# The fourth stick-breaking sample step, moved from the third attention pair's steps into the fourth pair's

## The chip, the cores and the metric

The kernel runs as one program on one core of a Trainium2 chip. The metric is the device time of one execution in microseconds (us); the kernel before was run three times, and its median is 1700.19 us.

## The reference, cut to what matters

One inference step of a hybrid encoder layer, for one prompt of 1024 rows and for eight samples of 16 rows with 512 cached positions each. All of it is float32, D_MODEL is 1024.

```
h = rmsnorm(x); z = h @ W_in
MLA, 8 heads:            softmax attention over latents, for samples over cache + own rows
retention, 4 heads
stick-breaking, 4 heads: log_beta = log_sigmoid(z), log_keep = log_sigmoid(-z) where key before query
                         between = reverse cumsum(log_keep) - log_keep
                         a = exp(log_beta + between); out = a @ v
x += concat(heads) @ W_out
x += memory cross-attention(rmsnorm(x))
x += ConvFFN(rmsnorm(x)); final rmsnorm
```

For the samples, stick-breaking runs over the caches `cache_sb_k` and `cache_sb_v`, and MLA over `cache_mla_ckv` (the latents) and `cache_mla_kpe` (the rotary keys).

## The kernel before, in words

**Stages.** The program runs in this order: the input projection with retention beside it, an attention stage written as numbered steps, the samples' latent attention, then the output projection, memory attention, ConvFFN and the last norm. The change lies in the attention stage, which ends at the latent attention.

**The steps.** `STEPS` (L212 to L223) is the one list from which every engine takes its order. It starts with ten "sb" steps, stick-breaking of the prompt. Then come four MLA pairs (two heads each), numbered 0 to 3 in the code and first to fourth here, of five steps each: `PACKS` names the tiles of 128 queries that one step takes, (7,), (6, 0), (5, 1), (4, 2), (3,). Between them stand four "sbs" steps. Each of these is the stick-breaking attention of two samples, for all heads, and takes one score tile where an MLA step takes two. `SB_S_AFTER` says behind which step of which pair each stands: `(2, 1): 3` puts the last one behind the second step of the third pair. The step numbers t of the attention stage are in the kernel before: 23 and 24 the third pair's first two, 25 the last sbs step, 26 to 28 the rest of the third pair, 29 to 33 the fourth pair.

**The pipeline over t.** TensorE's loop (L2609) does in turn t: the scores of step t, the transposes of the probabilities of t-1, the values of t-2. Between them it puts chunks of the next pair's projections (`STEP_CHUNKS`, L304; a pair has 11, spread over the four first MLA steps of the pair before; the fourth pair has none to place). An sbs step issues `sample_scores` (L2462, L2466) in turn t, five transposes (L2480) in turn t+1, `values` (L2497) in turn t+2, and in turn t+3 two transposes, `turn_sums` (L2512), and a wait for `sb_picked`. ScalarE takes the exponentials (L1143) or, for an sbs step, two sigmoids (L1134, L1135), each change of function with a table load; it copies the first group of every transposed head (L1154) and the outputs (L1166, L1170), and picks the turned sums (L1180). VectorE takes the row maxima and masks (L1742, L1745, L1736), the normalisation (L1767, L1771) or, for sbs, the scan and product (L1755, L1760), the second group's copy (L1782), and evacuates the query chunks (L1795).

**What is loaded where.** The sbs steps read their caches from four blocks of `z` (`cache_k`, `cache_v`; two transfers of 1 MB per step). The same blocks are later filled for the latent attention: `lat_v` of samples 2 to 7 and the rotary keys `lat_pe` of samples 0 to 3. The rest of the rotary keys goes where the projections' inputs were, and the latents `lat_k` and `lat_v` of samples 0 and 1 go into the buffers of the third pair. SyncE's queue (SP) issues all of these in one fixed order:

```
            sp.wait_ge(pv_done, SB_S_STEP[-1] + 1)
            for b in range(4):
                load_rotary(b)
            for b in range(2, DB):
                load_values(b)
            sp.wait_ge(proj_done, NCK * NP)
            ...
            sp.wait_ge(pv_done, END[NP - 2])
            for b in range(DB):
                sp.dma_start(lat_k[b], io["lat"][b, 0]).then_inc(lat_in[b], 16)
                if b < 2:
                    load_values(b)
```

`pv_done` counts the finished `values`, one per step, and `SB_S_STEP[-1]` is the number of the last sbs step. Where the "..." stands, the other four samples' rotary keys and `w_v` are issued. A `load_rotary` is two transfers (L850), a `load_values` one (L845), a `lat_k` one (L866). Behind them SP issues the first two weight blocks of the output projection (L761); GpSimd (POOL) splits a block into a high and a low part (L918, L921).

**Who needs them.** In turn t = N_STEPS = 34, `latent_scores(0)` (L2567, L2573) waits for `lat_in` of samples 0 and 1, 64 each, so for both samples' two rotary transfers, values and latents. TensorE takes this ahead of the values of step 32. `N_STEPS` stays 34 wherever an sbs step stands.

Of the kernel before, what the change touches and what calls it, by code (L numbers as in the profile page):

```python
# [207 lines left out]


PACKS = ((7,), (6, 0), (5, 1), (4, 2), (3,))  # L210
SB_S_AFTER = {(0, 2): 0, (1, 0): 1, (1, 3): 2, (2, 1): 3}
STEPS = [("sb", p, tiles) for p in range(2) for tiles in (PACKS[4:] + PACKS[:4] if p == 0 else PACKS)]  # L212
N_SB = len(STEPS)
FIRST, END, SB_S_STEP = [], [], []
for _i in range(NP):
    FIRST.append(len(STEPS))
    for _k, _tiles in enumerate(PACKS):
        STEPS.append(("mla", _i, _tiles))
        if (_i, _k) in SB_S_AFTER:
            SB_S_STEP.append(len(STEPS))  # L220
            STEPS.append(("sbs", SB_S_AFTER[_i, _k], (PAST // P,)))
    END.append(len(STEPS))
# [2843 lines left out]
```

## Time and profile before

| | |
|---|---|
| median of 3 runs | 1700.19 us (1700.18 to 1700.97) |
| the profiled execution's own time | 1700.53 us |
| its span in the trace | 1698.7 us |
| TensorE busy | 1673.5 us (99%) |
| VectorE, ScalarE, GpSimd busy | 1059.9, 530.7, 499.9 us |
| granted TensorE clock, mean | 0.999 |

The span runs from the first to the last instruction of the profiled execution; its own time is 1.8 us longer. "Busy" is the share in which an engine has an instruction under way. TensorE's matmuls overlap, so a matmul's duration is longer than the distance from its start to the next one's. In the tables, "idle before" is the time that an engine stood still ahead of an instruction, and the arrow names what ended it.

### The profile page before, as it was taken

The page shows a single profiled execution, that of the slowest core. Times are in us where ns is not written, and L with a number is a line of the kernel's source. Part 1 is how long each engine was busy: PE and PEld are TensorE (multiplying, and loading weights), DVE is VectorE, ACT ScalarE, POOL GpSimd, SP SyncE. Part 2 cuts the span into 40 slices and gives each one's busy share as a digit, 9 for nine tenths or more (in the row PEclk, how much of TensorE's full clock was granted, in tenths as well). Part 3 has the DMA queues.
Part 4 walks back from the last instruction along what each step waited for, and adds up shares of the span by engine and source line. Part 5 has one row for each costly group of instructions (what it writes and reads, how often), then busy time and mean ns, then how long its engine had stood idle before and what let it go on. Part 6 is the DMA issues. An engine that isn't in the chain of part 4 may idle for free.

```text
span 1698.7 us, 26502 instructions
## 1 busy us (share of the span) xinstructions
PE 1673.5 (99%) x10487; PEld 1544.3 (91%) x10487; DVE 1059.9 (62%) x1438; ACT 530.7 (31%) x960; POOL 499.9 (29%) x231
## 2 busy tenths in 40 slices
PE   9999999999999999999999999999999999999998
PEld 8899879766667799998999999999999999999997
DVE  7483477896666655446677656565655656565566
ACT  7220122586566541215333120211203021120222
POOL 2683142000000123420333333433334333343332
PEclk9999999999999999999999999999999999999999
DMA  5322121320222324316211111111111111111113
GB/s 207 92 86 81 52 69 38 110 75 24 77 86 69 113 78 138 107 38 266 90 38 50 38 47 39 37 49 37 48 38 37 49 37 49 37 37 49 38 47 112
DMA packets 36333, 119.41 MB, mean 70 GB/s; under 512 B 6048, under 2 KB 9344, under 8 KB 33952
## 3 DMA queue, kind: packets, MB, share of 16 engines
q1 hardware_dynamic: 33952, 108.89, 20.0%
q10 hardware_dynamic: 2304, 9.44, 1.6%
q8 instruction: 56, 0.92, 0.2%
q14 instruction: 21, 0.17, 0.0%
HBM read 100.86 MB, written 15.17 MB: 68 GB/s over the span
## 4 chain that ended last, share of the span: by engine, by line
PE 93%; DVE 3%; ACT 1%; issue 1%; POOL 1%; DMA 0%; SPq 0%; DVEq 0%; ACTq 0%; POOLq 0%
PE scores L2118 35%; PE bank L2118 35%; PE scores L2423 3%; PE bank L2480 3%; PE scores L2214 2%; PE bank L2504 2%; PE bank L2127 1%; PE scores L2136 1%; PE scores L2445 1%; PE bank L2534 1%; PE bank L2775 1%; PE bank L2538 1%; PE scores L2753 1%; PE bank L2497 1%; DVE kbuf L1755 1%
## 5 line engine op out<-in xcount | busy, mean ns | idle before, releaser
L918 POOL TENSOR_TENSOR w_hi<-w_raw,zero 128x1024 fp32r<-128x1024 f32 x96 | 187.4, 1952 | 1104.2 <-PE bank L2118 466.8
L2118 PE MATMUL scores<-act_hi,w_hi 128*128 128x384 f32 x920 | 310.2, 337 | 0.9 <-POOL w_lo L921 0.9
L2118 PE MATMUL scores<-act_lo,w_hi 128*128 128x384 f32 x920 | 309.1, 336 | 0.0
L2118 PE MATMUL scores<-act_hi,w_lo 128*128 128x384 f32 x920 | 309.1, 336 | 0.0
L921 POOL TENSOR_TENSOR w_lo<-w_raw,w_hi 128x1024 fp32r<-128x1024 f32 x96 | 252.5, 2631 | 7.5
L2046 DVE TENSOR_TENSOR x<-bank,x 128x384 f32<-128x384 f32 x216 | 120.5, 558 | 103.6 <-PE bank L2118 103.6
L2118 PE MATMUL bank<-act_hi,w_hi 128*128 128x384 f32 x544 | 183.7, 338 | 0.9 <-POOL w_lo L921 0.9
L2118 PE MATMUL bank<-act_hi,w_lo 128*128 128x384 f32 x544 | 182.8, 336 | 0.0
L2118 PE MATMUL bank<-act_lo,w_hi 128*128 128x384 f32 x544 | 182.8, 336 | 0.0
L2118 PEld LDWEIGHTS scores<-act_hi,w_hi 128*128 128x128 f32 x920 | 173.0, 188 | 2.5 <-POOL w_lo L921 1.5
L2118 PEld LDWEIGHTS scores<-act_lo,w_hi 128*128 128x128 f32 x920 | 173.0, 188 | 0.0
L2118 PEld LDWEIGHTS scores<-act_hi,w_lo 128*128 128x128 f32 x920 | 173.0, 188 | 0.0
L2020 DVE SCALAR_TENSOR_TENSOR conv<-ext,consts,conv 128x1168 f32<-128x1168 f32 x44 | 117.6, 2673 | 79.4 <-ACT conv L1421 79.4
L2118 PE MATMUL bank<-s_lo,w_hi 128*128 128x384 f32 (+2 forms) x454 | 152.7, 336 | 0.0
L2118 PE MATMUL bank<-s_hi,w_hi 128*128 128x384 f32 (+2 forms) x454 | 152.7, 336 | 0.0
L2118 PE MATMUL bank<-s_hi,w_lo 128*128 128x384 f32 (+2 forms) x454 | 152.6, 336 | 0.0
L1432 ACT ACTIVATE s_hi<-conv 128x1024 fp32r<-128x1024 f32 x20 | 21.2, 1060 | 344.2 <-DVE conv L2029 344.2
L2118 PEld LDWEIGHTS bank<-act_hi,w_hi 128*128 128x128 f32 x544 | 102.3, 188 | 2.1 <-POOL w_lo L921 1.2
L2118 PEld LDWEIGHTS bank<-act_lo,w_hi 128*128 128x128 f32 x544 | 102.3, 188 | 0.0
L2118 PEld LDWEIGHTS bank<-act_hi,w_lo 128*128 128x128 f32 x544 | 102.3, 188 | 0.0
L2022 DVE SCALAR_TENSOR_TENSOR conv<-ext,consts,conv 128x1168 f32<-128x1168 f32 x44 | 83.1, 1888 | 7.0 <-DVE conv L2020 4.2
L2118 PEld LDWEIGHTS bank<-s_hi,w_hi 128*128 128x128 f32 x454 | 85.3, 188 | 0.3
(402 smaller groups left out, 3101.2 us busy)
## 6 DMA issues: line engine op xcount, KB each, us to landing
w_raw<-wstream SPq DMA_DIRECT2D x106, 512.0 KB, 3.6
x_blk<-xT ACTq DMA_DIRECT2D x8, 576.0 KB, 4.7
x_mid<-x_blk ACTq DMA_DIRECT2D x8, 576.0 KB, 3.1
x<-x_mid SPq DMA_DIRECT2D x4, 1152.0 KB, 5.5
z<-cache_k SPq DMA_DIRECT2D x4, 1024.0 KB, 5.4
z<-cache_v SPq DMA_DIRECT2D x4, 1024.0 KB, 7.3
mk_c<-mk_c SPq DMA_DIRECT2D x4, 1024.0 KB, 11.7
mv_c<-mv_c SPq DMA_DIRECT2D x4, 1024.0 KB, 13.7
```

The lines of the kernel that those rows point to most:

```text
L918: pool.tensor_tensor(w_hi[:, k], w_raw[:, k], zero[:].unsqueeze(2).to_broadcast([P, KB, P]), ALU.add).then_inc(w_rounded, 1)
L921: pool.tensor_tensor(w_lo[:, k], w_raw[:, k], w_hi[:, k].bitcast(F32), ALU.subtract).then_inc(w_split, 1)
L1432: act.activation(dst[:, 0:TP], conv[:, 0, 0:TP], ACT.Copy)
L1755: own_v(dve.tensor_tensor_scan(keep[:, ::-1], keep[:, ::-1], ones[:, 0:1].to_broadcast([P, w]), 1.0, ALU.mult, ALU.mult))
L2020: own_v(dve.scalar_tensor_tensor(c, ext[:, ab, 1:EXT - 1], conv_tap(m + NFF * ab, 1), c, ALU.mult, ALU.add))
L2022: dve.scalar_tensor_tensor(c, ext[:, ab, 2:EXT], conv_tap(m + NFF * ab, 2), c, ALU.mult, ALU.add).then_inc(conv_done, 1)
L2046: dve.tensor_tensor(x[:, m, frames(c)], bank[6 + q % 2][:, 0:CH], x[:, m, frames(c)], ALU.add).then_inc(d_evac, 1)
L2118: mm = pe.matmul(out, w[:, k, at + kb], x(kb), start=first and kb == 0 and n == 0, stop=last and kb == n_kb - 1 and n == 2)
L2214: mm = pe.matmul(bank[c][:, 0:CH], w[:, 0, kb], x[:, at, frames(c)], start=i == 0 and n == 0, stop=i == KB - 1 and n == 2)
L2423: mm = pe.matmul(S[hh][:, at:end], q_pass[i % 2][:, hh, tile(j)], k_pass[i % 2][:, hh, at - first:end - first], start=True, stop=True)
L2480: mm = pe.transpose(bank[4 + g % 2][:, tile(b)], taken(t, hh)[:, tile(4 * k + b)], ident[:])
L2504: mm = pe.matmul(bank[6][64 * hh:64 * hh + 64, tile(n)], v, probT[:, t % 2, hh, at + P * b:at + P * b + P], start=b == 0, stop=b == j)
```

## The change

The last sbs step stands behind the second step of the fourth pair.

```diff
 PACKS = ((7,), (6, 0), (5, 1), (4, 2), (3,))
-SB_S_AFTER = {(0, 2): 0, (1, 0): 1, (1, 3): 2, (2, 1): 3}
+SB_S_AFTER = {(0, 2): 0, (1, 0): 1, (1, 3): 2, (3, 1): 3}
 STEPS = [("sb", p, tiles) for p in range(2) for tiles in (PACKS[4:] + PACKS[:4] if p == 0 else PACKS)]
```

With it `SB_S_STEP[-1]` goes from 25 to 30, `END[NP - 2]` from 29 to 28, and the steps from there are numbered: 25 to 27 the rest of the third pair, 28 and 29 the fourth pair's first two, 30 the sbs step, 31 to 33 the rest of the fourth pair. The two waits of SP that are quoted above are for `pv_done` at 31 and at 28, where they were for 26 and 29. Nothing else in the code is changed.

## Rows read from the trace of the kernel before

**Rows 1.** The page: engines, and the chain that ended last, by line.
```profile
PE 1673.5 (99%) x10487; PEld 1544.3 (91%) x10487; DVE 1059.9 (62%) x1438; ACT 530.7 (31%) x960; POOL 499.9 (29%) x231
PE 93%; DVE 3%; ACT 1%; issue 1%; POOL 1%; DMA 0%; SPq 0%; DVEq 0%; ACTq 0%; POOLq 0%
```

**Rows 2.** Windows: length, PE, PEld, DVE, ACT, POOL busy (instructions), PEclk, DMA share, GB/s.
```profile
538.50:572.40 33.90, 33.90 (x276) 24.75 (x273) 26.42 (x60) 20.43 (x53) 0.56 (x1) 1.00 0.51 164
572.40:603.00 30.60, 29.63 (x211) 21.29 (x209) 17.36 (x38) 16.06 (x36) 7.90 (x4) 1.00 0.13 35
603.00:700.00 97.00, 97.00 (x578) 96.11 (x577) 51.23 (x44) 24.39 (x27) 36.13 (x14) 1.00 0.38 124
```

**Rows 3.** TensorE's timeline around the sbs step: start, us, engine, line, operation.
```profile
504.49 0.45 PE L2538 MATMUL bank<-cq_hi,wq_hi 128*128 128x384 f32 x1 [0.27 <-ACT k_pass L1206]
...
509.48 1.10 PE L2480 MATMUL bank<-ident,prob 128*128 128x128 f32 x8 [0.34 <-ACT probT L1154]
...
521.24 1.16 PE L2545 MATMUL bank<-w_pass,z 128*128 128x128 f32 x8 [0.37 <-DVE q_pass L1795]
...
531.41 0.60 PE L2497 MATMUL bank<-sv_tok,probT 128*64 128x256 f32 x4
531.95 0.71 PE L2550 MATMUL bank<-q_pass,w_pass 64*128 64x128 f32 x4
...
533.55 0.38 PE L2512 MATMUL bank<-ident,probT 128*128 128x128 f32 x2
533.76 1.04 PE L2480 MATMUL bank<-ident,prob 128*128 128x128 f32 x8
```

**Rows 4.** ScalarE's timeline: the table loads on either side of the sigmoids.
```profile
509.36 1.28 ACT L1134 ACT_TABLE_LOAD   x1
...
516.86 1.28 ACT L1143 ACT_TABLE_LOAD   x1
```

**Rows 5.** SP's timeline: the loads in the order of their issue.
```profile
532.06 3.59 SPq L850 DMA_DIRECT2D z<-kpe_c  x8
535.68 2.79 SPq L845 DMA_DIRECT2D z<-lat  x6
538.52 3.68 SPq L850 DMA_DIRECT2D lat_pe<-kpe_c  x8
542.25 0.42 SPq L862 DMA_DIRECT2D w_v<-w_v  x1
...
552.34 0.43 SPq L866 DMA_DIRECT2D lat_k<-lat  x1
552.82 0.43 SPq L845 DMA_DIRECT2D lat_v<-lat  x1
553.29 2.97 SPq L866 DMA_DIRECT2D lat_k<-lat  x6
```

**Rows 6.** DMA issues: w_v; lat_k of sample 1; the last lat_k (size, us to landing).
```profile
w_v<-w_v SPq DMA_DIRECT2D x1, 256.0 KB, 4.3
...
lat_k<-lat SPq DMA_DIRECT2D x1, 256.0 KB, 3.5
...
lat_k<-lat SPq DMA_DIRECT2D x1, 256.0 KB, 6.1
```

**Rows 7.** TensorE's timeline from the last pair's last step to the first latent scores.
```profile
565.95 1.13 PE L2423 MATMUL scores<-k_pass,q_pass 128*128 128x512 f32 x2
...
572.44 1.02 PE L2567 MATMUL scores<-lat_k,q_abs 128*128 128x512 f32 x2
```

**Rows 8.** TensorE's first 32 matmuls (timeline); eight transposes of the fourth pair (chain).
```profile
1.09 5.52 PE L2184 MATMUL bank<-ones 128*128 128x128 f32 x32 [1.09 <-DVE eps L1480]
...
567.08 0.87 PE bank L2480 x8
```

**Rows 9.** GpSimd's first weight split; TensorE's first matmul that reads a split block.
```profile
571.85 1.89 POOL L918 TENSOR_TENSOR w_hi<-w_raw,zero 128x1024 fp32r<-128x1024 f32 x1 [263.86 <-DVE prob L1771]
...
602.95 0.60 PE L2214 MATMUL scores<-mix,w_hi 128*128 128x384 f32 x2
```

## The prediction

> **What bounds the kernel now.** I read the page first. TensorE is busy for 99% of the span and holds 93% of the chain that ended last, DMA 0% of it [rows 1]. So a microsecond taken from or added to TensorE's order is a microsecond of the end, unless TensorE was standing there anyway. The windows by stage come next [rows 2]: over the fourth pair, 538.5 to 572.4, TensorE is busy in all of 33.90 us. In the latent attention up to 603 it rests for 0.97 us of 30.60, and behind that not at all. Nothing after the changed place has a reserve that would swallow a delay. The fourth pair has no hole either, though it has no projection chunks: moving a step into it fills nothing.
>
> TensorE's timeline around the sbs step has the only rests near it: 0.27 us for an evacuated key chunk, 0.34 us between two transposes, 0.37 us for an evacuated query chunk [rows 3]. Last I read SP's timeline [rows 5]. The first load for the latent attention starts at 532.06, and the sbs step's values end at 531.41 + 0.60 = 532.01 [rows 3]. That end releases it, 0.05 us later. In the code this wait is `pv_done` at the last sbs step plus one.
>
> **The change part by part.** TensorE's instructions stay the same in number and shape: they move by five steps. So do the two sigmoids, their two table loads, the scan, the product and the copies.
>
> *1. The third pair without the sbs step.* The rest of 0.37 us at 521.24 lies behind the second of the table loads, 1.28 us at 516.86 [rows 3, 4]: ScalarE is late with the exponentials, VectorE with the normalisation behind them, and so with the query chunk. Without the step this goes. The rest of 0.27 us stands ahead of it and stays. I take -0.4 us; the bounds are 0 and -0.98, all three rests.
>
> *2. The fourth pair with it.* The 0.34 us belongs to the sbs turn itself, where two heads' transposes follow each other without scores between them, and moves along: 0. The table load back to the exponentials was followed by TensorE work on two projection chunks, which are missing there. What hides it is one head's scores and the values of step 29; my estimate, from the durations in the third pair, is that the exponential is just ready when TensorE asks. If not, it costs at most one table load, +1.28 us. I take 0. The turned sums and the wait for `sb_picked` fall in turn 33, after the release of the loads; a delay there is swallowed by term 3.
>
> *3. The loads behind the sbs step.* This is the large term. The release moves from turn 27 to turn 32, and with it everything behind it in SP's queue: eight rotary transfers, six of values, eight rotary, `w_v`, and then latents and values of samples 0 and 1, 27 transfers, before `latent_scores(0)` may start. The later wait, for the third pair's values, is then long met, so nothing pauses the queue.
>
> What TensorE still has to do behind the release: before, turn 33 and one head's transposes took 572.44 - 565.95 = 6.49 us [rows 7]; the turned sums add 533.76 - 533.55 = 0.21 us [rows 3]. The values end 0.06 us after the start of the next matmul (532.01 against 531.95). That leaves 6.64 us.
>
> What the loads need: `w_v` is issued 542.25 - 532.06 = 10.19 us after the first load and lands 4.3 us later, so at 14.5 us [rows 5, 6]. Up to there the sequence is the one of before. Four transfers of 256 KB follow. For their rate I take the second burst: `lat_k` of sample 1 landed at 552.34 + 3.5 = 555.8. The last `lat_k` was issued some 0.43 us before the end of its group of six, at 553.29 + 2.97 - 0.43 = 555.8, and landed 6.1 us later, at 561.9 [rows 5, 6]. Seven transfers in 6.1 us are 0.87 us each. So the fourth lands at 14.5 + 4 x 0.87 = 18.0 us. TensorE rests for 18.0 + 0.05 - 6.64 = **11.4 us**. It has rested nowhere near as long before.
>
> Bounds: the last of the four is issued at about 10.19 + 0.43 x 4 = 11.9 us at the earliest, and if it found the engines as free as sample 1's `lat_k` did (3.5 us) it would land at 15.4, a rest of 8.8 us. If all four ran as slowly as 1 us each, it would be 11.9 us. The value nearer to the upper end is the likelier, since `w_v` already took 4.3 us in a queue that was behind.
>
> *4. TensorE's clock after the rest.* No stretch of this trace has a rest of this length in mid-kernel, so the nearest row is the program's start: the first 32 matmuls of 128x128 took 5.52 us, where eight transposes of the same shape later take 0.87 us of the chain [rows 8], which is 3.5 us for 32. The difference is 2.0 us, though the granted clock of that stretch is given as 1.00. I take **+2.0 us** for the first matmuls behind the rest, which are as dense (latent scores, two steps' values). Bounds: 0, and twice the start's loss, 4.0.
> The Trainium skill, "TensorE: Matmul & The Clock Gate", section "Part 1: The HAM clock gate", says that the gate lets only half of the pulses through when the engine has been idle, and opens once it is busy again. By it the sum has this term; without it the sum would be 2.0 us lower.
>
> *5. What lies further back.* SP's output-projection weights were issued from 556.65 on. In the changed queue they stand behind six more `lat_k`; at 0.87 us for each 256 KB the first 512 KB have landed 18.0 + 8 x 0.87 = 25.0 us after the first load, which starts at 572.44 - 6.64 + 0.05 = 565.85, so at 590.9. GpSimd's first split, which before started at 571.85 on a VectorE result, waits for them. TensorE asks for a split block at 602.95 + 11.4 = 614.4 [rows 9]. Between the two lie 23 us, for a split of which the first half takes 1.89 us: 0. The latents of samples 2 and 3 land 1.7 us behind, while TensorE has the scores of two samples and the values of two steps to do: 0. All later loads hang on TensorE's progress and move with it.
>
> **Sum.** -0.4 + 0 + 11.4 + 2.0 = +13.0 us. The profiled execution took 1700.53 us (span 1698.7 and 1.8 around it), the median is 1700.19, 0.3 lower. From the median this gives 1713.2 us, 0.8% slower. A measurement of this kernel can tell about 0.2%, 3.4 us, from no change.
>
> **The rivals.**
> *A, the clock does not fall* (chance 0.18). The rest is there, but the engine comes back at full rate. For it speaks that the granted clock reads 1.00 in every stretch, even where the first matmuls were slow. Against it, those slow matmuls themselves. 1700.2 - 0.4 + 11.4 = 1711.2 us.
> *B, the fourth pair misses its cover* (0.06). The exponentials behind the sigmoids come a table load too late, and the sums' turn too: up to 1.3 us and a rest of 0.4 us more, with the clock term 1715.0. For it speaks the thin cover in term 2; against it, that the same steps in the third pair rested only where a projection chunk asked.
> *C, not slower: the loads come in time* (0.05). The place is the wait of `latent_scores(0)`. It decides from the point where the fourth 256 KB transfer lands within 6.64 us of the release; then only term 1 is left, 1700.2 - 0.4 = 1699.8, at most 1699.2. Issuing 27 transfers took SP about 12 us of its own time in the trace, so this needs a release that does not move, a change that does not do to SP's queue what the code says. The 0.05 us between the values' end and the first load speaks against that.
> The forecast itself, stall and slow start together, has 0.71.
>
> **The numbers.** The predicted time is the forecast's, 1713.2 us. The range takes in rival A, with the earlier landing (rest 9.6 instead of 11.4: 1709.4), and on the other side rival B with a somewhat slower clock return (1716.5). I set 1709.0 to 1716.5. The rest of 0.2 is C and the corners of the bounds. Slower by over 0.2% are the forecast, A and B: 0.95. Within 0.2% is nearly all of C: 0.04. Faster by over 0.2% has no mechanism: 0.01.
>
> **What the profile after would show.** SP's first rotary load should start about 34 us later, near 565.5, with no pause between `w_v` and the first `lat_k`. TensorE's latent scores should show an idle time of about 11 us ahead of them, released by a DMA, and start near 583.5; the step should be the largest wait of TensorE in the whole trace. The matmuls behind it should be about twice as far apart for some microseconds. The rest of 0.37 us behind the sigmoids should be gone from the third pair, and from 603 on every stage should have its length of before. The forecast is wrong if the idle time ahead of the latent scores is under 8 us, if another wait of over 1 us appears in the fourth pair, or if the first output-projection matmul waits for a weight split.

## The result, and the profile after

The changed kernel takes 1713.26 us (median of 5 runs, 1712.75 to 1714.78), the kernel before, measured beside it, 1700.39 us (1700.18 to 1700.97). The ratio is 1.0077, with a 95% interval from 1.0063 to 1.0091: 12.9 us slower. 1713.2 was forecast.

The profiled execution of the changed kernel is the slowest of the five, at 1714.78 us with a span of 1713.0; against the profiled one of before that is 14.25 us. The page, first its span, then the lines of [rows 1]:

```profile
span 1713.0 us, 26502 instructions
PE 1675.1 (98%) x10487; PEld 1545.5 (90%) x10487; DVE 1061.2 (62%) x1438; ACT 530.5 (31%) x960; POOL 500.0 (29%) x231
...
PE 92%; DVE 3%; ACT 1%; issue 1%; SPq 1%; POOL 1%; DMA 1%; DVEq 0%; ACTq 0%; POOLq 0%
```

The counts are those of before; TensorE's busy time is 1.6 us more, which the low clock below accounts for. What is new is SP's queue and the DMA in the chain that ended last, with 1% each. TensorE's three largest waits in the changed kernel, by their sum (what was waited for: us in all, times, the longest):

```profile
PE scores L2567 <- DMA lat_v<-lat: 12.6, 1, 12.6
PE bank L2480 <- ACT probT L1154: 2.2, 5, 0.9
PE scores L2118 <- POOL w_lo L921: 1.7, 2, 0.9
```

One wait explains nearly all. Its place in TensorE's timeline, from the last sbs step's values to the latent scores (answers to [rows 3] and [rows 7]):

```profile
563.02 1.95 PE L2497 MATMUL bank<-z,probT 128*64 128x256 f32 x16
564.80 0.60 PE L2497 MATMUL bank<-sv_tok,probT 128*64 128x256 f32 x4
565.33 1.12 PE L2423 MATMUL scores<-k_pass,q_pass 128*128 128x512 f32 x2
...
571.17 1.09 PE L2480 MATMUL bank<-ident,prob 128*128 128x128 f32 x8
584.88 2.05 PE L2567 MATMUL scores<-lat_k,q_abs 128*128 128x512 f32 x2 [12.61 <-DMA lat_v<-lat]
586.72 0.63 PE L2567 MATMUL scores<-z,q_abs 128*128 128x128 f32 x2
587.28 1.95 PE L2573 MATMUL scores<-z,q_pe 64*128 64x512 f32 x8
```

And SP's timeline, the answer to [rows 5]:

```profile
565.44 4.05 SPq L850 DMA_DIRECT2D z<-kpe_c  x8
569.53 3.71 SPq L845 DMA_DIRECT2D z<-lat  x6
573.29 3.67 SPq L850 DMA_DIRECT2D lat_pe<-kpe_c  x8
577.01 0.42 SPq L862 DMA_DIRECT2D w_v<-w_v  x1
577.47 0.43 SPq L866 DMA_DIRECT2D lat_k<-lat  x1
577.95 0.43 SPq L845 DMA_DIRECT2D lat_v<-lat  x1
578.42 0.43 SPq L866 DMA_DIRECT2D lat_k<-lat  x1
578.89 0.43 SPq L845 DMA_DIRECT2D lat_v<-lat  x1
```

The values end at 564.80 + 0.60 = 565.40, the first load starts 0.04 us later, and 27 loads go out without a pause, where before there were 8.8 us between `w_v` and the first `lat_k`. The last stretch of the chain in order of time shows where the latest of them landed, 578.89 + 5.74 = 584.63:

```profile
578.89 5.74 DMA lat_v<-lat
584.63 0.25 issue
584.88 2.47 PE scores L2567 x4
```

The windows over the rest and behind it, columns as in [rows 2] (the seventh is the granted clock):

```profile
565.00:572.00 7.00, 7.00 (x66) 5.13 (x62) 5.37 (x14) 4.55 (x16) 0.00 (x0) 1.00 0.47 127
572.00:583.00 11.00, 0.26 (x3) 0.03 (x1) 0.00 (x0) 0.95 (x2) 0.00 (x0) 0.63 0.95 279
584.00:585.00 1.00, 0.12 (x1) 0.15 (x1) 0.00 (x0) 0.00 (x0) 0.00 (x0) 0.50 1.05 383
587.00:588.00 1.00, 1.00 (x4) 0.56 (x5) 0.00 (x0) 0.00 (x0) 0.00 (x0) 0.50 1.04 416
588.00:589.00 1.00, 1.00 (x8) 0.46 (x4) 0.00 (x0) 0.00 (x0) 0.00 (x0) 0.74 1.10 430
589.00:590.00 1.00, 1.00 (x22) 0.88 (x20) 0.70 (x2) 0.00 (x0) 0.00 (x0) 1.00 0.61 238
```

The clock fell to 0.50, that is 1.2 of 2.4 GHz, while TensorE stood still. It reads 0.74 on average between 588 and 589, so it came back at about 588.5, when the engine had been at work again for 3.6 us. Half of these 3.6 us is the loss: from the first latent scores to the values of step 32 it took 589.16 - 584.88 = 4.28 us; before it was 574.90 - 572.44 = 2.46.

The difference of the two profiled executions adds up. The latent scores start 12.78 us later than by the distance of before (0.93 us behind the transposes at 571.17). The low clock costs 1.82. The stretch between the last two old landmarks, the query chunk behind the rest of 0.27 us and the last step's transposes, is shorter by 0.91 (571.51 - 504.49 = 67.02 before, 571.17 - 505.06 = 66.11 after). And the attention stage begins 0.57 us later (505.06 against 504.49), which lies ahead of anything that was changed. 12.78 + 1.82 - 0.91 + 0.57 = 14.26 us. Nothing is left over for the stages behind. TensorE's waits from 700 us on are the same six in both traces, 3.9 us in all.

### The profile page after: what moved, and what is told of

It reads as the page before. It is cut to its first block, busy times and chain, and to the rows that moved or that the text cites. A ratio compares the mean times of both kernels' runs of the same rounds, so it can differ in the third digit from the quotient of the medians.

```text
span 1713.0 us, 26502 instructions
## 1 busy us (share of the span) xinstructions
PE 1675.1 (98%) x10487; PEld 1545.5 (90%) x10487; DVE 1061.2 (62%) x1438; ACT 530.5 (31%) x960; POOL 500.0 (29%) x231
## 4 chain that ended last, share of the span: by engine, by line
PE 92%; DVE 3%; ACT 1%; issue 1%; SPq 1%; POOL 1%; DMA 1%; DVEq 0%; ACTq 0%; POOLq 0%
PE scores L2118 35%; PE bank L2118 35%; PE scores L2423 3%; PE bank L2480 2%; PE scores L2214 2%; PE bank L2504 2%; PE bank L2127 1%; PE scores L2136 1%; PE scores L2445 1%; PE bank L2534 1%; PE bank L2538 1%; PE bank L2775 1%; PE scores L2753 1%; PE scores L2567 1%; PE bank L2497 1%
## 5 line engine op out<-in xcount | busy, mean ns | idle before, releaser
L1432 ACT ACTIVATE s_hi<-conv 128x1024 fp32r<-128x1024 f32 x20 | 21.2, 1060 | 344.1 <-DVE conv L2029 344.1
## 6 DMA issues: line engine op xcount, KB each, us to landing
mv_c<-mv_c SPq DMA_DIRECT2D x4, 1024.0 KB, 13.7
```

Of the source, the lines that this page charges most:

```text
L1432: act.activation(dst[:, 0:TP], conv[:, 0, 0:TP], ACT.Copy)
```

## The experiments

The theory: the whole loss hangs on SP's queue, since the loads of the latent attention wait behind the last sbs step. The rivals: the sbs step costs something in its new place by itself; the clock is not what makes the first latent scores slow; the bytes, not their order, decide. All times are medians. The kernel before, measured beside each, had 1700.35 to 1700.42 us.

### The loads that are free go first

```diff
-            sp.wait_ge(pv_done, SB_S_STEP[-1] + 1)
-            for b in range(4):
-                load_rotary(b)
-            for b in range(2, DB):
-                load_values(b)
             sp.wait_ge(proj_done, NCK * NP)
             ...
+            sp.wait_ge(pv_done, SB_S_STEP[-1] + 1)
+            for b in range(4):
+                load_rotary(b)
+            for b in range(2, DB):
+                load_values(b)
```

The "..." stands for the free loads, which are unchanged: rotary keys of samples 4 to 7, `w_v`, then all `lat_k` and the `lat_v` of samples 0 and 1.

> The changed kernel, with SP's order altered: the loads that don't use the cache blocks (rotary keys of samples 4 to 7, w_v, all lat_k, lat_v of samples 0 and 1) are issued ahead of the wait for the last sbs step, the rest behind it. Theory (the cost is SP's queue behind one wait): behind the release only four rotary transfers are needed for the first latent scores; they land some 3.7 us after it, within the 6.6 us that TensorE still works. No wait on a DMA, no drop of the clock, and only the local gain stays: 1699.5 us, from 1699.2 to 1700.4. Rival (the sbs step in the fourth pair costs by itself): well above 1700.4. Rival (the amount of data behind the release decides): 1705 or more.

Measured: 1699.99 us (1699.36 to 1703.49, 11 runs), ratio 1.0001 [0.9992, 1.001]. The 12.9 us are gone with the sbs step still in the fourth pair: TensorE's timeline has the latent scores at 571.24, with no idle time ahead of them. That is the theory's result, and both rivals fall for this place. But seven runs lie at 1699.4 to 1700.1 and four at 1701.0 to 1703.5, so something else costs now and then. The profiled run (1701.04) shows it. VectorE's and GpSimd's timelines of this kernel:

```profile
579.33 2.66 DVE L1894 TENSOR_SCALAR prob<-prob,row_sum 128x640 f32<-128x640 f32 x1
...
584.21 2.32 DVE L1894 TENSOR_SCALAR prob<-prob,row_sum 128x640 f32<-128x640 f32 x1
...
588.74 0.55 DVE L1894 TENSOR_SCALAR prob<-prob,row_sum 128x640 f32<-128x640 f32 x1
```

```profile
577.32 1.89 POOL L918 TENSOR_TENSOR w_hi<-w_raw,zero 128x1024 fp32r<-128x1024 f32 x1 [269.61 <-DMA w_raw<-wstream]
579.29 2.35 POOL L921 TENSOR_TENSOR w_lo<-w_raw,w_hi 128x1024 fp32r<-128x1024 f32 x1
581.59 2.15 POOL L918 TENSOR_TENSOR w_hi<-w_raw,zero 128x1024 fp32r<-128x1024 f32 x1
583.82 2.35 POOL L921 TENSOR_TENSOR w_lo<-w_raw,w_hi 128x1024 fp32r<-128x1024 f32 x1
```

The two long normalisations start 0.04 and 0.39 us after a GpSimd instruction does (579.29 and 583.82) and end 0.35 us after that one ends (581.99 against 581.64, 586.53 against 586.17). The other five of the seven meet no split; the third shown takes 0.55. TensorE waited 1.8 us for the two in all. In the kernel before, GpSimd started at 571.85 [rows 9] and was done at 580.46, just before the first of the seven, and each of them took 0.55. Here the weights are issued behind the released loads, the split starts 5.5 us later and falls into the normalisations. The Trainium skill, "SBUF — State Buffer", section "SBUF: two separate sides", says that VectorE and GpSimd share one pair of ports as an exclusive lock: a GpSimd instruction, and a VectorE instruction in a two-port mode or with two inputs from SBUF (then only beside a GpSimd instruction that reads SBUF), shut each other out for the whole instruction of the one that starts first. The trace agrees in the times: the end of each long instruction follows the end of GpSimd's, and GpSimd's next one, which begins while the first of them is still under way, takes 2.15 us instead of 1.89. Whether the normalisation runs in such a mode, no row here shows.

### Only the release moves

```diff
-            sp.wait_ge(pv_done, SB_S_STEP[-1] + 1)
+            sp.wait_ge(pv_done, 31)
```

> The kernel before, with one number changed: SP's wait ahead of the first rotary load is for pv_done at 31 instead of 26. The sbs step stays in the third pair. Theory: the queue alone makes the loss. TensorE waits about 12 to 13 us for the latents (19.2 us from release to landing as in the changed kernel, 6.4 us of work left), the clock term of 1.8 comes on top, and the local gain of 0.9 is missing: 1714.3 us, from 1712.5 to 1715.5. Rival (the sbs step's new place costs): 1700.4.

Measured: 1714.37 us (1713.49 to 1715.31), ratio 1.0083 [1.0068, 1.0099]. The step stood in its old place and the loss was there, 1.1 us more of it than in the changed kernel; the local gain of 0.9 us is missing here. It is the reverse of the first experiment; together they show the queue to be both enough and necessary. The wait of the profiled run:

```profile
582.59 2.05 PE L2567 MATMUL scores<-lat_k,q_abs 128*128 128x512 f32 x2 [10.47 <-DMA lat_v<-lat]
```

It is shorter than the 12 to 13 us expected, and the low clock behind it cost 2.52 us, not 1.8 (the table further down), so the time agrees with the expectation in part by luck.

### TensorE kept busy through the rest

```diff
+                if t == N_STEPS:
+                    pe.wait_ge(kv_evac, evacuated(NP - 1, NCK - 1, "act"))
+                    for _ in range(90):   # 45 in the second kernel
+                        pe.matmul(bank[7][:, 0:P], ident[:], ones[:], start=True, stop=True)
                 if t >= N_STEPS:
                     latent_scores(t - N_STEPS)
```

> The changed kernel, with 90 matmuls of 128x128 (identity by ones, into a free bank, read by nothing) ahead of the first latent scores: about 9.8 us of TensorE's rest of 12.6 us are filled. Theory (the first matmuls behind the rest are slow because the clock fell): the latent scores start when they did, the granted clock stays 1.00, and from there to the values of step 32 it takes 2.5 us instead of 4.3: 1.8 us less, 1711.4 us. Rival (they are slow for another reason, as data that still arrives): 1713.3.

Measured: 1719.54 us (1719.04 to 1720.06), far from the 1711.4 expected. I had taken one float32 matmul for one instruction, and it is two: 90 became 180 and filled more than the rest.

```profile
571.20 20.26 PE L2624 MATMUL bank<-ones,ident 128*128 128x128 f32 x180
591.29 1.02 PE L2567 MATMUL scores<-lat_k,q_abs 128*128 128x512 f32 x2
```

The time says nothing on the question, but the trace does: the clock read 1.00, and from these latent scores to the next values it took 2.46 us, as before the change. The second kernel had half of the filling.

> The changed kernel with 45 instead of 90 of the filling matmuls. With 90 the trace had 180 instructions of 0.11 us each, 20.3 us, longer than the rest itself, so the time said nothing; 45 take 10.1 us and leave about 2 us of the rest of 12.6. Theory (the clock had fallen): the latent scores start when the last needed transfer has landed, as in the changed kernel, the granted clock stays 1.00, and from them to the values of step 32 it takes 2.5 us instead of 4.3: 1711.4 us, 1.8 us less. Rival (the first matmuls are slow because transfers still run beside them, or the start after any rest costs that): 1713.3.

Measured: 1712.17 us (1711.66 to 1713.28), ratio 1.0069 [1.0055, 1.0083]: 1.1 us less than the changed kernel, where 1.8 were expected. Its trace:

```profile
571.36 10.21 PE L2624 MATMUL bank<-ones,ident 128*128 128x128 f32 x90
583.23 1.10 PE L2567 MATMUL scores<-lat_k,q_abs 128*128 128x512 f32 x2 [1.66 <-DMA lat_v<-lat]
...
597.68 0.77 PE L2655 MATMUL bank<-ident,prob 128*128 128x128 f32 x5 [0.95 <-DVE prob L1894]
```

The latent scores still waited for the DMA, and behind that wait they ran at full rate: 585.76 - 583.23 = 2.53 us to the values, against 4.28. Transfers still ran beside them (the DMA share was 1.04 from 583 to 585), so these do not slow TensorE, nor does a wait of 1.66 us; in the changed kernel, where the same stretch was slow, the clock read 0.50. In the profiled run a part of the gain was given back by the meeting of VectorE and GpSimd, 0.95 us.

### All behind the release, in the order of need

```diff
             sp.wait_ge(pv_done, SB_S_STEP[-1] + 1)
-            for b in range(4):
-                load_rotary(b)
-            for b in range(2, DB):
-                load_values(b)
-
             sp.wait_ge(proj_done, NCK * NP)
-            for b in range(4, DB):
-                load_rotary(b)
-            sp.dma_start(w_v[:], io["w_v"]).then_inc(sample_in, 16)
-
             sp.wait_ge(pv_done, END[NP - 2])
             for b in range(DB):
+                load_rotary(b)
                 sp.dma_start(lat_k[b], io["lat"][b, 0]).then_inc(lat_in[b], 16)
-                if b < 2:
-                    load_values(b)
+                load_values(b)
+            sp.dma_start(w_v[:], io["w_v"]).then_inc(sample_in, 16)
```

> The changed kernel, all loads still behind the last sbs step's values, but sample by sample (rotary, latents, values), w_v last. The bytes behind the release are the same. Theory (what counts is what stands ahead of the fourth needed transfer): eight transfers instead of 27, issued in 3.7 us and landed 7 to 8 us after the release; a rest of 0 to 1.5 us, no drop of the clock, 1700.5 us, from 1699.4 to 1702. Rival (the bytes in all decide): the rest stays near 12 us and the time at 1713.

Measured: 1704.67 us (1702.38 to 1707.45, 11 runs), ratio 1.0024 [1.0015, 1.0033]. The two waits that matter, from TensorE's timeline:

```profile
572.31 1.10 PE L2559 MATMUL scores<-lat_k,q_abs 128*128 128x512 f32 x2 [0.86 <-DMA lat_v<-lat]
...
598.31 1.33 PE L2643 MATMUL bank<-ident,prob 128*128 128x128 f32 x5 [4.80 <-DVE prob L1886]
```

The first is as expected, 0.9 us where 12.6 were, with the same bytes behind the same release: the order decides, not the amount. The time missed the expectation (1699.4 to 1702). In the profiled run, at 1707.36 one of the longest, the second wait is the reason. The weights came last in this order too, GpSimd split from 588.06 to 597.89, and two normalisations (L1886 here) took 2.14 and 2.31 us; VectorE's instruction on `mixed` between them took 3.50 us instead of 1.35. And TensorE's clock fell in this wait too, though no DMA was waited for:

```profile
603.00:604.00 1.00, 1.00 (x5) 0.51 (x5) 0.00 (x0) 0.00 (x0) 0.00 (x0) 0.55 0.00 0
```

It reads 0.50 from 598 to 603. From the transposes behind the wait to the next ones TensorE took 605.13 - 598.31 = 6.82 us, where the same stretch took 4.67 in the kernel before: 2.15 us on top of the 4.8.

### The step one turn earlier, two earlier, one later

```diff
-SB_S_AFTER = {(0, 2): 0, (1, 0): 1, (1, 3): 2, (3, 1): 3}
+SB_S_AFTER = {(0, 2): 0, (1, 0): 1, (1, 3): 2, (3, 0): 3}   # and (2, 4), and (3, 2)
```

> The last sbs step behind the fourth pair's first step, one turn earlier than in the changed kernel. Theory: the release comes one turn, 7.3 us, earlier; TensorE's rest shrinks from 12.6 to 5.3 us, the clock still falls (1.8 us): 1700.4 - 0.9 + 5.3 + 1.8 = 1706.6 us, from 1704.5 to 1707.5. Rival (the place in the fourth pair costs, not the loads): as the changed kernel, 1713.

> The last sbs step behind the third pair's last step, two turns earlier than in the changed kernel. Theory: some 21 us of TensorE's work lie behind the release, more than the 19.2 us that the loads take: no rest, 1700.0 us, from 1699.4 to 1701. If the local gain of 0.9 us comes from leaving the projection chunks, it shows here, unless this place has a wait of its own.

> The last sbs step behind the fourth pair's third step, one turn later than in the changed kernel. Theory: about 1 us of work is left behind the release, a rest of about 18.3 us, the clock term as before: 1719.6 us, from 1718 to 1721. Rival (the rest is bound by something that doesn't move with the release): 1713.

Measured, with the profiled runs' numbers (start of the first load; idle time ahead of the latent scores; from the first load to the latent scores; what the stretch from these to the second value group, 5.63 us before, took more; how long of it the granted clock read 0.50):

| last sbs step behind | first load | idle | load to scores | slower by | at 0.50 | median |
|---|---|---|---|---|---|---|
| (2, 4) | 551.14 | 0 | 21.2 | 0 | 0 | 1700.65 (1700.18 to 1701.07) |
| (3, 0) | 557.92 | 3.89 | 17.95 | 2.83 | 5.8 | 1706.96 (1706.03 to 1707.75) |
| (3, 1), the change | 565.44 | 12.61 | 19.44 | 1.82 | 3.6 | 1713.26 |
| (3, 2) | 570.66 | 16.25 | 18.00 | 2.47 | 5.1 | 1719.77 (1719.53 to 1719.92) |
| (2, 1), late release | 565.58 | 10.47 | 17.01 | 2.52 | 5.2 | 1714.37 |

The price of the clock is in every row half of the time that it stood at 0.50, to within 0.1 us, and does not follow the length of the rest. The windows in which it came back, of (3, 0), (3, 2) and the late release (the seventh column is its mean over half a microsecond):

```profile
581.50:582.00 0.50, 0.50 (x12) 0.50 (x10) 0.47 (x1) 0.00 (x0) 0.50 (x1) 0.84 0.08 33
593.50:594.00 0.50, 0.50 (x10) 0.50 (x10) 0.37 (x2) 0.00 (x0) 0.00 (x0) 0.78 0.39 131
587.50:588.00 0.50, 0.50 (x9) 0.50 (x10) 0.43 (x2) 0.00 (x0) 0.00 (x0) 0.75 0.97 385
```

All three medians came within 0.7 us of what was expected, but the parts did not: behind (3, 0) a rest of 5.3 us and 1.8 for the clock were expected and 3.89 and 2.83 came, behind (3, 2) 18.3 and 1.8 against 16.25 and 2.47. Waits that nobody had counted made up for it in part. Beside the moved sbs step TensorE waited 0.40 us for ScalarE's sigmoids and 0.40 for VectorE behind (3, 0), and behind (3, 2) 0.55 us for VectorE's copy and 0.48 for ScalarE's. So these places do cost something by themselves, which (3, 1) did not.

Where TensorE waits for the loads, these need 17 to 19.4 us from release to scores, and the time rises with what is missing of them. Behind (2, 4) there is work enough. Its time has no gain over the kernel before: the rests of 0.34 and 0.37 us [rows 3] are gone there, but three new ones stand beside the sbs step, 0.96 us for ScalarE's sigmoids, 0.40 for VectorE's product and 0.35 for an exponential. One line each from the waits of these kernels, (3, 0) first, and of (2, 4), where 0.4 of the 1.4 us is an older wait at 443.73 that the kernel before has too:

```profile
PE scores L2567 <- DMA lat_v<-lat: 3.9, 1, 3.9
```

```profile
PE scores L2423 <- ACT prob L1135: 1.4, 2, 1.0
```

### The order of the first experiment without the move

The same edit of SP's order as in the first experiment, on the kernel before.

> The kernel before with SP's order of the first experiment, so that this order is tested without the move. Theory: the loads were in time before and still are, 1700.4 us within 0.5. Compared with the first experiment it gives what the move alone brings where no load is late: 0.9 us less there.

Measured: 1700.33 us (1700.25 to 1700.72, 11 runs), ratio 1.0001 [0.9992, 1.001]. The order by itself does nothing. In the kernel before, the release came long before the loads were wanted. Against the first experiment, where only the step's place differs, the medians are 0.3 us apart and not the 0.9 expected; the four long runs of the first experiment take a part of it away.

### Free loads and weights ahead of the wait

To the first experiment's kernel:

```diff
+            sp.wait_ge(q_evac, evacuated(NP - 1, NCK - 1, "dve"))
+            stream(W_OUT, W_OUT + 2)
             sp.wait_ge(pv_done, SB_S_STEP[-1] + 1)
...
-            sp.wait_ge(q_evac, evacuated(NP - 1, NCK - 1, "dve"))
-            stream(W_OUT, W_OUT + 4)
+            stream(W_OUT + 2, W_OUT + 4)
```

> The kernel of the first experiment, with the first two weight blocks of the output projection also issued ahead of the wait for the last sbs step. In the first experiment they came last, GpSimd's split ran from 577.3 to 586.1 instead of from 571.9 to 580.5, and two of VectorE's normalisations (L1894) took 2.66 and 2.32 us instead of 0.55, for which TensorE waited 1.8 us. Theory: the split is back at its old place relative to the latent scores, the two instructions take 0.55 us, and the local gain of 0.9 us shows whole and in every run: 1699.5 us, with a spread under 1 us where the first experiment had 1699.4 to 1703.5. Rival (the spread comes from the loads' landing): spread as in the first experiment.

Measured: 1699.63 us (1699.18 to 1700.34, 11 runs), beside 1700.42 for the kernel before (1700.09 to 1700.94, 15 runs); ratio 0.9995 [0.9986, 1.0004]. GpSimd's first split is back behind VectorE's last normalisation of the fourth pair:

```profile
571.01 1.89 POOL L919 TENSOR_TENSOR w_hi<-w_raw,zero 128x1024 fp32r<-128x1024 f32 x1 [262.87 <-DVE prob L1772]
```

The runs above 1700.4 are gone, and the spread is 1.2 us where it was 4.1. Only the place of the weights was changed, so the long runs hang on it; that VectorE and GpSimd met in them is seen in the one that was profiled and is argued for the others. The median is 0.8 us below the kernel before, and it is what the 0.9 us of the traces would give; the interval still reaches over 1, so it is a likely gain, not a sure one.

## Why the prediction was right

**The release (term 3, its mechanism).** Right in each part: the 0.05 us from the values to the first load (0.04), SP's pause-free queue, the work of 6.64 us left to TensorE (from 565.44 to where the scores could have started, 571.17 + 0.93, 6.66), and the wait at `latent_scores(0)`. Two experiments, the loss without the move and the move without the loss, carry it.

**How much of the hit is luck.** Forecast and median agree to 0.1 us, which is closer than the terms do. In the profiled run the rest was 1.4 us longer than forecast by the distance (12.78 against 11.4), the clock 0.2 and the local term 0.5 lower, 13.7 us in all against 13.0. The median lies 12.9 us above the kernel before, but no trace of such a run was kept, so how its terms divide is open.

**The size of the rest (11.4 us, measured 12.6 in the profiled run).** This lies outside the bounds of 8.8 and 11.9 that the term was given, since the upper one held `w_v`'s landing fixed. `w_v` was issued 11.57 us after the first load, not 10.19: one of SP's rotary issues took 0.88 us and one of the values 1.34, where about 0.45 is usual. It landed 3.4 us later, at 15.0 (forecast 14.5), and the four transfers behind it took 4.2 us, 1.05 each instead of 0.87. From the last landing to the scores it took 0.25 us, not 0.05. Over four other traces the way from the first load to the scores was 17.0 to 18.5 us, forecast 18.05; so the estimate held for the middle of the runs, and the profiled run was at the slow end. Its own time is 1.5 us above the median.

**The clock (2.0 us, measured 1.8).** The mechanism was right. The size is partly luck: it was taken from the program's start, where the granted clock reads 1.00, and not from a time at half rate, which was 3.6 us here and 5.1 to 5.8 in three other kernels, where the same stretch took 2.5 to 2.8 us more. The bound of 4.0 was needed. The rule of the Trainium skill that I had set beside this term ("TensorE: Matmul & The Clock Gate", "Part 1: The HAM clock gate") holds here in both directions, 1.00 to 0.50 in the rest and back in the work behind it. Rival A falls with the 0.50 of the windows and with the filled rest.

**The local gain (-0.4 us, measured -0.9).** This term was mis-sized by the most for its size. The rest of 0.37 us went as said, and those of 0.27 and 0.34 stayed as said. What I had not counted is how TensorE's pieces follow each other. Pieces of the chain before the change, and of the chain after it:

```profile
505.82 1.87 PE scores L2462 x8
512.48 1.92 PE scores L2423 x6
535.66 1.05 PE bank L2480 x8
```

```profile
506.38 1.72 PE scores L2423 x6
529.13 0.87 PE bank L2480 x8
544.72 1.72 PE scores L2462 x8
```

The sample scores took 1.87 us behind a projection chunk and 1.72 behind values (0.15). Scores of an MLA step took 1.92 us behind values, 1.72 behind a chunk, and one step fewer stands directly behind values (0.20). The second head's transposes in the last step of the third pair took 1.05 before and 0.87 after (0.18). With the 0.37 that is 0.90. Why the transposes came closer was not tried.

**The fourth pair's cover (term 2, 0 us) and rival B.** The exponentials behind the second table load were in time. No new wait of TensorE over 0.4 us stands there; only the 0.34 moved along.

**What lies further back (term 5, 0 us).** True for the changed kernel, as the sum of the terms shows: nothing is left over for it. But "0" was not safe. GpSimd's split moved to 590.08 (forecast for its data 590.9, a near hit by luck: the needed transfers were slower than assumed, and the eight times 256 KB behind them faster, 0.68 us each), and one of VectorE's normalisations took 1.81 us beside it. It cost TensorE nothing that run, up to 4.8 us in an experiment. I had asked only whether the weights come in time, not what their later arrival meets.

**Rival C** fell with the release at 565.44.

**Two figures that don't follow from the rows.** The range's lower end uses a rest of 9.6 us for an earlier landing, where the bound worked out above it was 8.8 (1708.6 instead of 1709.4), and rival B's parts add up to 1714.9, not 1715.0. Neither touches the forecast.

## What to carry to other kernels

A step's place in a pipeline also sets when its buffers come free, and a queue that issues in a fixed order holds up everything behind that one wait, needed or not. Before a step is moved later, count what the queue must still issue and land between the release and the first reader, and set that against the work left on the busy engine; if it falls short, put ahead of the wait whatever doesn't need it. Loads that move can also move another engine's work into a place where it blocks a third: look at who runs beside it.

## What was not expected of the hardware

- The first scores behind a rest of 3.9 us were as slow as behind one of 16.2 us (2.83 and 2.47 us more in the same stretch). A wait of 3.9 us cost 6.7 in all.
- A VectorE normalisation of 0.55 us takes up to 2.66 beside a GpSimd split, and the runs of that kernel spread from 1699.4 to 1703.5 us, which went away when the weights, and with them the split, came earlier.
- A float32 matmul stands in the trace as two instructions; 45 of 128x128 took 10.2 us.
- SP's issues are mostly 0.42 us long, but single ones took 0.88 and 1.34. What makes them long, and why the same four transfers need 1.05 us each in one run and less in others, was not tried and stays open.
